# RWKV output norm: v centred when it is turned, square sums inside the chunk loop, head rows spread by fp32r products, first panels fed chunk by chunk

## What is computed

```python
S, y = scan over tokens of:  sa = S @ a_t
                             S = S * w_t + sa b_t^T + v_t k_t^T
                             y_t = S @ r_t                 # 16 heads of 64
mu = mean(y, over the head);  var = mean((y - mu)**2, over the head)
y = (y - mu) * rsqrt(var + 64e-5) * gn_w + gn_b
bonus = sum(r * k * r_k, over the head) * v
y_rwkv = ((y + bonus) * g) @ w_rwkv_out                    # g = sigmoid(xg @ g1) @ g2
merged = sigmoid(z_rwkv) * y_rwkv + sigmoid(z_conv) * y_conv
x = x + rms_norm(merged @ w_out) ...                       # then an FFN
```

## Time and profile before

| | |
|---|---|
| time, median of 3 runs | 2477.31 us (2476.69 to 2480.69) |
| profiled execution | 2476.06 us, of which the span from first to last instruction 2474.3 us |
| mean granted TensorE clock | 0.98 of full speed |
| TensorE busy | 95% of the span; weight load 80% |
| VectorE, ScalarE, GpSimd busy | 42%, 37%, 41% |
| chain that ended last | TensorE 89%, VectorE 3%, issue 3%, GpSimd 2%, ScalarE 2% |

### The profile page before, as it was taken

The page is one execution under the profiler, slowest core; times in us unless marked ns, Lnnn a source line. Parts: engine busy times, 40 slices in busy tenths (PEclk is TensorE's granted clock), DMA queues, the critical chain, the costliest instruction groups (busy, mean ns, idle before and its releaser), DMA issues.

```text
span 2474.3 us, 41463 instructions
## 1 busy us (share of the span) xinstructions
PE 2362.1 (95%) x17492; PEld 1974.2 (80%) x17492; DVE 1050.7 (42%) x1509; ACT 903.5 (37%) x1527; POOL 1017.9 (41%) x574
## 2 busy tenths in 40 slices
PE   6999999999899999999999999999898999999998
PEld 6878788888787878888877888676888877888886
DVE  6164622211456453221146988266333475322212
ACT  5165432322425643332243223545233344322322
POOL 3342544444545054444463444344000255444443
PEclk8999999999999999999999999989999999999998
DMA  6600243333441023333333333323000322333331
GB/s 167 139 26 22 85 115 94 102 93 95 99 103 52 9 77 94 102 95 96 94 95 115 99 94 103 110 77 111 4 4 4 127 74 74 101 95 95 96 96 63
DMA packets 384265, 210.27 MB, mean 85 GB/s; under 512 B 36415, under 2 KB 378151, under 8 KB 383827
## 3 DMA queue, kind: packets, MB, share of 16 engines
q1 hardware_dynamic: 378899, 188.36, 27.1%
q0 software_dynamic: 4512, 18.09, 1.9%
q10 hardware_dynamic: 672, 1.18, 0.1%
HBM read 196.72 MB, written 12.41 MB: 85 GB/s over the span
## 4 chain that ended last, share of the span: by engine, by line
PE 89%; DVE 3%; issue 3%; POOL 2%; ACT 2%; DMA 0%; ACTq 0%; POOLq 0%; DVEq 0%
PE ps L1841 24%; PE ps L1842 24%; PE ps L1843 24%; PE ps L2215 3%; PE ps L1944 2%; PE ps L1924 2%; PE ps L2182 2%; PE ps L2202 2%; PE ps L1933 1%; POOL x_res L686 1%; PE ps L1800 1%; DVE h_lo L1274 1%; PE ps L2229 1%; ACT w_hi L790 0%; DVE h_lo L1259 0%
## 5 line engine op out<-in xcount | busy, mean ns | idle before, releaser
L623 POOL TENSOR_TENSOR w_lo<-raw,w_hi 128x1024 fp32r<-128x1024 f32 (+2 forms) x344 | 810.7, 2358 | 1041.3 <-ACT w_hi L790 1040.8
L1841 PE MATMUL ps<-h_hi,w_hi 128*128 128x512 f32 x2016 | 799.0, 396 | 31.5 <-ACT h_hi L866 12.9
L1842 PE MATMUL ps<-h_hi,w_lo 128*128 128x512 f32 x2016 | 791.3, 392 | 0.0
L1843 PE MATMUL ps<-h_lo,w_hi 128*128 128x512 f32 x2016 | 791.0, 392 | 0.0
L790 ACT ACTIVATE w_hi<-raw 128x1024 fp32r<-128x1024 f32 (+2 forms) x344 | 356.9, 1038 | 1173.0 <-PE ps L1843 1172.1
L1841 PEld LDWEIGHTS ps<-h_hi,w_hi 128*128 128x128 f32 x2016 | 383.0, 190 | 127.7 <-issue 43.6
L1843 PEld LDWEIGHTS ps<-h_lo,w_hi 128*128 128x128 f32 x2016 | 382.5, 190 | 81.1
L1842 PEld LDWEIGHTS ps<-h_hi,w_lo 128*128 128x128 f32 x2016 | 383.4, 190 | 78.1
L1841 PE MATMUL ps<-hid_hi,w_hi 128*128 128x512 f32 x528 | 205.4, 389 | 0.0
L1842 PE MATMUL ps<-hid_hi,w_lo 128*128 128x512 f32 x528 | 205.4, 389 | 0.0
L1843 PE MATMUL ps<-hid_lo,w_hi 128*128 128x512 f32 x528 | 205.4, 389 | 0.0
(11 more groups left out here) (315 smaller groups left out, 2810.5 us busy)
## 6 DMA issues: line engine op xcount, KB each, us to landing
raw<-in_w_gu SPq DMA_DIRECT2D x88, 512.0 KB, 3.9
raw<-in_w_in SPq DMA_DIRECT2D x56, 512.0 KB, 3.8
raw<-in_w_down SPq DMA_DIRECT2D x32, 448.0 KB, 3.9
raw<-in_w_out SPq DMA_DIRECT2D x24, 512.0 KB, 4.2
raw<-in_ffn_w_gate SPq DMA_DIRECT2D x22, 512.0 KB, 3.9
raw<-in_ffn_w_up SPq DMA_DIRECT2D x22, 512.0 KB, 3.9
raw<-in_w_in_b SPq DMA_DIRECT2D x20, 512.0 KB, 3.9
raw<-in_w_down SPq DMA_DIRECT2D x16, 512.0 KB, 4.1
```

The lines of the kernel that those rows point to most:

```text
L623: nc.gpsimd.tensor_tensor(lo[:, k0:, :], src[:, k0:, :], hi[:, k0:, :].bitcast(f32), ALU.subtract).then_inc(lo_done, 1)
L1841: nc.tensor.matmul(bank, wh[:, k, :], ah[:, 0:width], start=first, stop=False)
L1842: nc.tensor.matmul(bank, wl[:, k, :], ah[:, 0:width], start=False, stop=False)
L1843: return nc.tensor.matmul(bank, wh[:, k, :], al[:, 0:width], start=False, stop=end)
```

## The change

- `masks` gets an eleventh matrix, I - 1/64, and the "v" products use it in place of the identity: v arrives centred in the chunk loop. u_v itself stays as it is for the bonus.
- ScalarE squares each "ys" product into u_k before it copies it to u_r. New products "sums" add the squares over heads for 128 tokens each: three in the last round of the list, the fourth behind it.
- The root and reciprocal of the norm are done once for 48 and once for 16 columns, not chunk by chunk. The statistics are turned into rows (16 heads x 512 tokens) and split into rows_hi and rows_lo; `spread_of_heads` spreads two heads with 2 fp32r products against a picking matrix `pick`. The bonus uses it too, with its rows made by a new product "rows" in round 3.
- The bias gn_b is added to u_v on GpSimd, and so is the sum of scaled y and bonus.
- GpSimd's loads of conv, z_rwkv and z_conv are issued in three groups, the first two ahead of the last "ys". ScalarE waits for them by pairs of chunks.
- GpSimd splits w_lo one panel further ahead in the merge (c + 3).
- `first_two` becomes `pair_start` and `pair_chunk`; the norm's loop on TensorE issues a chunk of the pair three steps behind its spread.

The diff, cut to its core:

```diff
+    lists.append(np.eye(C) - 1.0 / HD)
...
+            if j == NC // 2 - 1:
+                beside[6] = [("rows", 0)]
...
-                    products += [x0, ("bk", (j - 1, 0)), ("bk", (j - 1, 1)), u0, ("bonus", 0), ys0, ("bonus", 1), x1,
-                                 ("bonus", 2), u1, ("bonus", 3), ys1]
+                    products += [x0, ("bk", (j - 1, 0)), ("bk", (j - 1, 1)), u0, ("bonus", 0), ("sums", 0),
+                                 ys0, ("bonus", 1), ("sums", 1), x1, ("bonus", 2), ("sums", 2), u1, ("bonus", 3), ys1]
...
-            product_out(pool, "ys", NC - 1)
             for par in range(2):
                 pool.wait_ge(sg[f"z_out{par}"], 16 * 3 * KD // 2)
+            product_out(pool, "bk", (NC // 2 - 1, 1))
             for c in range(KD):
-                pool.dma_start(u_kk[:, c, :], scratch["z"][c]).then_inc(sg["merge_in"], 16)
-                pool.dma_start(u_w[:, c, :], scratch["z"][KD + c]).then_inc(sg["merge_in"], 16)
-                pool.dma_start(u_b[:, c, :], scratch["conv"][c]).then_inc(sg["merge_in"], 16)
+                pool.dma_start(u_b[:, c, :], scratch["conv"][c]).then_inc(sg[f"merge_in{c // 2}"], 16)
+            for c in range(KD):
+                if c % 2 == 0:
+                    product_out(pool, "bonus", c // 2)
+                if c == 6:
+                    product_out(pool, "x", NC - 1)
+                    for k in range(KD):
+                        pool.dma_start(u_kk[:, k, :], scratch["z"][k]).then_inc(sg[f"merge_in{k // 2}"], 16)
+                nc.gpsimd.tensor_scalar(u_v[:, c, :], u_v[:, c, :], vec("gn_b_2", c), None, ALU.add
+                                        ).then_inc(sg["bonus_ready"], 1)
+            product_out(pool, "ys", NC - 1)
+            for c in range(KD):
+                pool.dma_start(u_w[:, c, :], scratch["z"][KD + c]).then_inc(sg[f"merge_in{c // 2}"], 16)
             pool.dma_start(x_res[:, :, :], scratch["x"]).then_inc(sg["x_in_again"], 16)
+            pool.wait_ge(sg["bonus_ready"], KD)
             for c in range(KD):
-                split_lo(L["rwkv_out"].p0 + c + 2)
+                pool.wait_ge(sg["y_scaled"], c + 1)
+                nc.gpsimd.tensor_tensor(u_r[:, c, :], u_r[:, c, :], u_v[:, c, :], ALU.add).then_inc(sg["y_bonus"], 1)
+            for c in range(KD):
+                split_lo(L["rwkv_out"].p0 + c + 3)
...
+            nc.scalar.activation(eps[:, 7:8], eps[:, 0:1], ACT.Sqrt)
...
+                        y = ps[:, bank, :].rearrange("p (c n) -> p c n", n=C)
+                        nc.scalar.activation(u_k[:, :, i * C:(i + 1) * C], y, ACT.Square).then_inc(sg["y_sq"], 1)
+                        nc.scalar.activation(u_r[:, :, i * C:(i + 1) * C], y, ACT.Copy).then_inc(bank_out[bank], 1)
+                    if kind == "rows":
+                        act.wait_ge(sg["product_done"], 2 * m + half + 1)
+                        rows_high(bank, 2 * half, 2 * half + 2)
+                    if kind == "sums":
+                        act.wait_ge(sg["product_done"], 2 * m + half + 1)
+                        k = 16 * i + 8 * half
+                        nc.scalar.activation(y_var[:, k:k + 8], ps[:, bank, 0:8], ACT.Copy).then_inc(bank_out[bank], 1)
...
+            product_out(act, "sums", 2)
+            nc.scalar.activation(y_var[:, 0:48], y_var[:, 0:48], ACT.Sqrt, scale=1.0 / HD, bias=eps[:, 2:3]
+                                 ).then_inc(sg["y_std"], 1)
+            act.wait_ge(sg["y_sums"], 1)
+            nc.scalar.activation(y_var[:, 48:64], ps[:, Y_SUM_BANK, 0:16], ACT.Sqrt, scale=1.0 / HD, bias=eps[:, 2:3]
+                                 ).then_inc(sg["y_std"], 1)
+            for bonus in range(NC // 2):
+                product_out(act, "bonus", bonus)
+            act.wait_ge(sg["y_rows"], 1)
+            rows_high(Y_ROW_BANKS[0], 0, 3)
+            act.wait_ge(sg["y_rows"], 2)
+            rows_high(Y_ROW_BANKS[1], 3, 4)
+            for c in range(KD):
+                act.wait_ge(sg["t_ready"], n["t"] + c + 1)
+                nc.scalar.activation(h_hi[:, c, :], u_r[:, c, :], ACT.Copy).then_inc(hh, 1)
+                if c == 6:
+                    split_hi_half("rwkv_out")
             n["t"] += KD
-            split_hi_half("rwkv_out")
-            act.wait_ge(sg["merge_in"], 16 * 3 * KD)
             for c in range(KD):
                 if c == 5:
                     split_hi(L["rwkv_out"].p0 + 4)
+                if c % 2 == 0:
+                    act.wait_ge(sg[f"merge_in{c // 2}"], 16 * 6)
...
+            dve.wait_ge(sg["w_sig"], KD)
+            for i in range(2):
+                nc.vector.tensor_copy(pick[i][:, :, :], ident[0:16, 8 * i:8 * i + 8].unsqueeze(2).broadcast_to([16, 8, HD])
+                                      ).then_inc(sg["pick_ready"], 1)
...
+            for k, (c0, c1) in enumerate(((0, 48), (48, 64))):
+                dve.wait_ge(sg["y_std"], k + 1)
+                nc.vector.reciprocal(y_rstd[:, c0:c1], y_var[:, c0:c1]).then_inc(sg["y_rec"], 1)
+            for k, (j0, j1) in enumerate(((0, 3), (3, 4))):
+                dve.wait_ge(sg["rows_hi"], 3 + k)
+                nc.vector.tensor_tensor(rows_lo[:, j0 * P:j1 * P], ps[0:16, Y_ROW_BANKS[k], j0 * P:j1 * P],
+                                        rows_hi[:, j0 * P:j1 * P].bitcast(f32), ALU.subtract).then_inc(sg["y_rows_lo"], 1)
             product_out(dve, "ys", NC - 1)
-            for c in range(KD + 4):
...
+                    dve.wait_ge(sg["y_spread"], c + 1)
+                    nc.vector.scalar_tensor_tensor(u_r[:, c, :], u_r[:, c, :], vec("gn_w_2", c), ps[:, Y_SPREAD_BANKS[c % 2], :],
+                                                   ALU.mult, ALU.mult).then_inc(sg["y_scaled"], 1)
+                if 1 <= c < KD + 1:
+                    k = c - 1
+                    dve.wait_ge(sg["y_bonus"], k + 1)
                     dve.wait_ge(sg["gate_done"], k + 1)
-                    nc.vector.tensor_tensor(y, y, ps[:, GATE_BANKS[k % 2], :], ALU.mult).then_inc(sg["t_ready"], 1)
-                if c >= 5:
-                    low_of_y(c - 5)
+                    nc.vector.tensor_tensor(u_r[:, k, :], u_r[:, k, :], ps[:, GATE_BANKS[k % 2], :], ALU.mult
+                                            ).then_inc(sg["t_ready"], 1)
+                if 2 <= c < KD + 1:
+                    low_of_y(c - 2)
...
+            def spread_of_heads(c, bank):
+
+                two = pick[c // 4][:, 2 * (c % 4):2 * (c % 4) + 2, :].rearrange("p e n -> p (e n)")
+                nc.tensor.matmul(ps[:, bank, :], two, rows_hi[:, :], start=True, stop=False)
+                return nc.tensor.matmul(ps[:, bank, :], two, rows_lo[:, :], start=False, stop=True)
...
+                                work = [(1 - cb, u_v[rows, c, tokens(i, cb)], masks[rows, M_CENTER, :]) for cb in range(2)]
...
+                    elif kind == "rows":
+                        pe.wait_ge(sg["rk_kept"], 1)
+                        for t4 in (2 * half, 2 * half + 1):
+                            last = nc.tensor.matmul(ps[0:16, bank, t4 * P:(t4 + 1) * P], rk_stat[:, 16 * t4:16 * t4 + 16],
+                                                    ident[:, :], start=True, stop=True)
                     elif kind == "bonus":
-                        pe.wait_ge(sg["rk_kept"], 1)
-                        k = 8 * (2 * i + half)
-                        for t4 in range(NT):
-                            for e in range(2):
-                                last = nc.tensor.matmul(ps[side(e), bank, t4 * P:(t4 + 1) * P],
-                                                        rk_stat[:, k + 2 * t4 + e:k + 2 * t4 + e + 1].broadcast_to([P, HD]),
-                                                        ident[:, :], start=True, stop=True)
+                        if half == 0:
+                            pe.wait_ge(sg["pick_ready"], 2)
+                            product_out(pe, "rows", 0)
+                        last = spread_of_heads(2 * i + half, bank)
+                    elif kind == "sums":
+                        if half == 0:
+                            pe.wait_ge(sg["y_sq"], 2 * i + 2)
+                        for c in range(4 * half, 4 * half + 4):
+                            last = nc.tensor.matmul(ps[:, bank, 2 * (c % 4):2 * (c % 4) + 2], u_k[:, c, i * P:(i + 1) * P],
+                                                    head_ones[:, 0:P:HD], start=True, stop=True)
...
+                if c >= 2:
+                    pe.wait_ge(sg["t_ready"], T_GATE + c - 1)
+                else:
+                    bank_clear(pe, GATE_BANKS[c])
                 nc.tensor.matmul(ps[:, GATE_BANKS[c % 2], :], g2[:, c * P:(c + 1) * P], lora_g[:, :], start=True, stop=True
                                  ).then_inc(sg["gate_done"], 1)
 
+            def rows_of_rstd(j0, j1, k):
+                bank_clear(pe, Y_ROW_BANKS[k])
+                pe.wait_ge(sg["y_rec"], k + 1)
+                for j in range(j0, j1):
```

(79 more changed lines are left out.)

73 lines of the change are left out of this document (19 added, 54 removed).

## The result

The changed kernel takes 2491.8 us (median of 4 runs, 2489.9 to 2499.1) beside 2477.0 us for the kernel before on the same chip: ratio 1.0068, 95% interval 1.0049 to 1.0087. The same two kernels on another chip gave 2495.6 and 2476.4 us, ratio 1.0083 (1.0061 to 1.0105). It is slower by 15 to 19 us between medians, 17 to 20 by the ratios. The forecast was 2480.0, range 2470 to 2487, so the time lies outside the range.

The account below looks back on a forecast made before the run. TensorE, busy 97 of 103.5 us, was taken to bound the stretch. Terms: -1.5 us by events, +2.7 clock in out2, +1.5 clock in the norm, so +2.7 on the median 2477.31: 2480.0 us, range 2470 to 2487.

Parts of the forecast that it names:

- Chunk loop, first rounds: Chunk loop: "rows" adds 0.4 us; the pick copies, between 0 and 1.4, cost 0 under a TensorE wait.
- Last round: Tail of the chunk loop: smaller bonus spreads save 4.0 us, three "sums" add 5.2; plus 1.2, at most 1.4.
- The bound of the square sums: Price taken from the old norm, 0.87 us for 4 products; a "sums" step of 8 products costs 1.74.
- Norm: Output norm and paired panels: the pair ends 32.3 us after the last ys product, before 45.6; gain 11.6 with the loop.
- the clock term: Clock loss in the new norm where TensorE does little: 1.5 us, bounds 0 and 2.7.
- The lap: Norm with pair chunks: TensorE's spread, gate and pair chunk take 2.8 us per chunk and bound; VectorE's take 2.6.
- the norm does not shrink: Rival: spreads and pair chunks wait for each other, lap near 4 us; 2489 us, chance 0.05.
- Moved bias and GpSimd: Norm: behind transfer issues and bias additions on GpSimd, the first bonus addition starts 10.0 us after the last ys product.
- GpSimd is late: Rival in the norm: slower issues or additions delay the first gated chunk; 2484 us, chance 0.23.
- The ring's lap: Merge: splitting w_lo at c + 3 closes a ring of gating, addition, m_hi, w_hi, w_lo; 6.05 us a panel against TensorE's 5.45.
- the stand in out2: Out2's first panel: TensorE waits 4.6 us for m_lo, before 0.33; slow clock behind it adds 2.7.
- the ring does not bind: Rival in the merge: stalls of about 4 us go and the clock holds; 2471 us, chance 0.22.

Follow-up runs that it names:

- e1: The changed kernel with GpSimd's w_lo split in the merge back at c + 2, as in the kernel before: 2483.2 us, ratio to before 1.0022.
- w1: The changed kernel with its 24 two-column square-sum products in the last round replaced by 512-column fp32r products on other data: 2483.1 us, ratio to before 1.0031.
- b2: The kernel before with 24 added fp32r products of 512 columns, results unused, at the places of 'sums': 2483.2 us, ratio 1.0024.
- n1: The changed kernel with idle 512-column fp32r products for TensorE added in the norm alone: 2492.8 us, ratio to before 1.0054.
- b1: The kernel before with 24 added two-column products on u_k, results unused, at the places of 'sums': 2489.4 us, ratio 1.0048.
- v5: v3 with old bonus spreads, panel 4's w_hi and w_lo earlier, and 384 tokens' square sums, root and reciprocal before the last ys product: 2463.0 us.
- v3: v1 with idle 512-column fp32r products added where TensorE waits in the norm: 2470.2 us, ratio to before 0.9963.
- v1: The changed kernel with square sums as 16 wide products behind the list, fewer GpSimd loads, and w_lo and w_hi reordered in the merge: 2472.7 us.
- e4: The changed kernel with 6 of 24 square-sum products left in the last round and the bonus spread by 8 fp32 products as before: 2480.6 us.

## Why the prediction was wrong, point by point

- **Chunk loop, first rounds: right, within noise.** The state update ahead of the last round moved by 4.6 us, of which 3.9 were there before the change. 0.7 stands against 0.4 for "rows" and 0 for the pick copies; but the same rounds are 2.4 us shorter in e1 (198.4 from the clearing of the state, 200.8 in the changed kernel), so one execution can't tell 0 from 1.2.
- **Last round: this step failed.** I wrote "the tail is TensorE-bound, so plus 1.2, at most 1.4". It is TensorE-bound, and it took 13.2. I priced every product at full clock, from rows of stretches where the clock was 1.00, and put clock losses only where TensorE would wait. In w1, at full clock, the round costs 3.2 us more than before, so 2.0 of the error is size: the added products cost 1.0 more than forecast (6.2 in b2, not 5.2), and the spreads saved 1.0 less (3.0 from b2 to w1, not 4.0). The other 8 to 10 us come from the clock, which falls when two-column products stand beside 16-row spreads. The prediction's sign for an error in the tail, the loop's end moving by more than 3 us, came true.
- **The bound of the square sums** was taken from the norm before, where the same products ran at full clock. But there they stood among head sums and gate products of 512 columns. The row gave the duration and not what its neighbours did for the clock (that they did something is argued from w1 and b2, no run changes them in the norm). The earlier trace rows had the warning, 0.56 behind small sums; I used it for the norm alone.
- **Norm: the structure was right in the main, the clock term too small.** Forecast 32.3 us from T' to the pair's end; n1, with its added products, took 34.6 at clock near 1.0. In the changed kernel it is 41.2: the clock term, set at 1.5 between bounds 0 and 2.7, was 6.6 or more. The upper bound came from 13 slow products behind a wait, but this stretch has half clock for 24 us (1975.5 to 1999). The lap, forecast at 2.8, is 3.1 us at full clock (pair chunks start at 2000.88, 2003.99, 2007.09), just past the 3 that was named as a sign of being wrong. The rival "the norm does not shrink" lies nearest to the time (2489), but by luck: the norm did shrink, by 4.3 us, and the lap is not 4.
- **Moved bias and GpSimd: right.** GpSimd was through with its issues at T' + 9.3 (forecast 10.0) and then waited 4.0 us for VectorE's first scaling, late because the spreads began at T' + 11.0 (forecast 6.0; 8.5 in n1, at full clock with added products). The rival "GpSimd is late" (2484) fell. The low halves beside GpSimd's additions took 1.39 us in place of 0.68, as the earlier trace rows let expect.
- **Merge: right.** The ring's lap 6.12 (6.05), the stand before panel 2's second half 2.6 (2.8), the stand in out2 4.3 (4.6) with slow products behind it. In all the merge lost 10.7 us, more than the norm had won; the forecast had 10.1 + 2.7. Inside it the terms are off both ways: the waits come to 8.8 us (forecast 11.8), and the clock also fell behind the stand before panel 2's second half (8 products at 0.43 us, 1.6 us), where the forecast had no clock term. e1 shows the cause of most of it. The rival "the ring does not bind" (2471) fell.
- **Sum.** Forecast +2.7. By events +20.3, without the 3.9 ahead of the change: 12.2 too little in the loop, 7.5 too little in the norm, 2.1 too much in the merge. No rival held a clock loss in a stretch where TensorE is busy, and so the range ended below the time.

What stays open: why two-column products cost 0.4 us more than wide ones beside the old spreads (in the one execution of b1 that was profiled) but 8 to 10 us more beside the 16-row ones, and whether it is their width or their number type. The runs show that both kinds are needed for the long fall, not what the chip weighs.

## What to carry to other kernels

In this kernel a product of TensorE had two prices: its duration, and what it did to the clock of its neighbours. Before small products (two columns, or few rows) are put into a stretch that runs at full clock, ask what wide work stands around them, and give the clock a rival of its own where the engine is busy, too; here the same sums as wide products with a narrow selecting weight cost less and, beside the old spreads, left the last round at full clock (v5: 30.2 us, 1.00). And an order that takes one step more ahead on a shared engine is to be followed round through every queue until it comes back to itself: if it does, the lap is the pace.

## What the runs showed of the hardware

- The granted clock fell to 0.5 with TensorE busy 40.4 of 41.9 us, the products being narrow: a busy engine is no sign of a full clock. Exchanging 24 fp32 products of two columns for wide fp32r ones of the same duration brought it to 1.00 (w1). The Trainium skill (TensorE: Matmul & The Clock Gate, "HAM oscillation — how this bites in real kernels") tells of the fall as what gaps between groups of products bring; in this trace it also falls with no gap ahead of it: TensorE had 1.5 us of idle time in the whole round, and none in the 4 us before the fall. Where the two differ, the measurement decides.
- Products that compute nothing, put in TensorE's waits, kept the clock at 0.99 to 1.00 over the 20 us behind the last round and more than paid for themselves in the norm's length (n1: 34.6 us in place of 41.2; v3: 32.2 in place of v1's 35.8). In w1 and e4, with the clock at 1.00 up to the last round's end, the norm fell to 0.74 by itself.
- VectorE's reciprocal goes by columns, not by elements: as rows of 16 partitions, 384 and 128 columns took 3.35 us together (v3), the longest step between the last squares and the first spread there. The changed kernel has as many elements, 8192, as 128 rows of 48 and 16 columns, and took 0.44 and 0.25 us.

```profile
1956.03 3.35 DVE L1775 RECIPROCAL y_row<-y_row 16x384 f32<-16x384 f32 x2 [0.69 <-ACT y_row L1226]
1959.31 0.73 DVE L1778 TENSOR_TENSOR rows_lo<-y_row,rows_hi 16x384 fp32r<-16x384 f32 x2
```

- A transfer issue on GpSimd costs little more for four chunks than for one: 1.55 us for two of four chunks (v3), 4.38 for eight of one (changed kernel), so 0.78 against 0.55 each.
